# Low parts of the feed-forward's middle activations on DVE instead of GpSimd, in a two-layer decoder step

## What is computed

```python
def _swiglu(x, w_i, w_o):
    h = jnp.einsum('btd,df->btf', x, w_i)
    gate, up = h[..., :D_FF], h[..., D_FF:]
    return jnp.einsum('btf,fd->btd', jax.nn.silu(gate) * up, w_o)
...
yp = _layernorm(ALPHA * yp + 0.5 * _swiglu(yp, ffn1_wi[l], ffn1_wo[l]), ln_g[l, 0], ln_b[l, 0])
```

## Time and profile before

| | us |
|---|---|
| median of 3 runs | 1996.91 (1996.44 to 1997.46) |
| the profiled execution | 1998.58 |
| its span in the trace | 1996.8 |

### The profile page before, as it was taken

The page is one execution under the profiler, slowest core; times in us unless marked ns, Lnnn a source line. Parts: engine busy times, 40 slices in busy tenths (PEclk is TensorE's granted clock), DMA queues, the critical chain, the costliest instruction groups (busy, mean ns, idle before and its releaser), DMA issues.

```text
span 1996.8 us, 36337 instructions
## 1 busy us (share of the span) xinstructions
PE 1866.5 (93%) x14532; PEld 1786.2 (89%) x14532; DVE 1257.3 (63%) x1871; ACT 880.1 (44%) x1377; POOL 455.4 (23%) x340
## 2 busy tenths in 40 slices
PE   7999989999989869899999999999999689999996
PEld 7999989996966549899999999999998589999995
DVE  5888852446957413888872368888324788887223
ACT  4455531343334422655562264555513375556223
POOL 3000072151321344300026230000721430002520
PEclk9999999999989979899999999999999789999998
DMA  5333363271100223233333223333233123333221
GB/s 164 85 105 105 105 242 101 70 180 43 45 2 1 54 74 107 60 89 105 105 101 101 88 72 87 103 105 105 96 101 94 28 64 99 101 101 111 84 75 43
DMA packets 260087, 179.80 MB, mean 90 GB/s; under 512 B 10847, under 2 KB 256999, under 8 KB 259462
## 3 DMA queue, kind: packets, MB, share of 16 engines
q1 hardware_dynamic: 249952, 154.90, 26.6%
q0 software_dynamic: 2288, 13.54, 1.9%
q10 hardware_dynamic: 7742, 9.88, 1.8%
HBM read 169.62 MB, written 8.08 MB: 89 GB/s over the span
## 4 chain that ended last, share of the span: by engine, by line
PE 78%; DVE 8%; issue 7%; ACT 4%; POOL 2%; DMA 1%; ACTq 0%; POOLq 0%; DVEq 0%
PE ps L1116 39%; PE ps L1023 28%; PE ps L1203 3%; PE ps L1044 1%; DVE w_lo L1619 1%; PE ps L1208 1%; ACT w_hi L604 1%; PE ps L1093 1%; ACT xf L633 1%; ACT xh L631 1%; PE ps L1187 1%; POOL k_sel L2319 1%; PE ps L1282 1%; DVE xf L1651 1%; POOL diag L2331 1%
## 5 line engine op out<-in xcount | busy, mean ns | idle before, releaser
L1619 DVE TENSOR_TENSOR w_lo<-w_raw,w_hi 128x2048 fp32r<-128x2048 f32 (+1 forms) x70 | 183.8, 2628 | 286.7 <-ACT w_hi L604 286.7
L2267 POOL TENSOR_TENSOR hl<-hid_all,hh 128x520 fp32r<-128x520 f32 x88 | 134.3, 1562 | 850.2 <-ACT hh L889 850.2
L1023 PE MATMUL ps<-hh,w_hi 128*128 128x260 f32 x1408 | 295.2, 285 | 5.3 <-DVE w_lo L1619 5.3
L1023 PE MATMUL ps<-hh,w_lo 128*128 128x260 f32 x1408 | 293.8, 284 | 0.0
L604 ACT CAST w_hi<-w_raw 128x2048 fp32r<-128x2048 f32 (+1 forms) x70 | 126.2, 1804 | 247.5 <-PE ps L1023 229.9
L1023 PEld LDWEIGHTS ps<-hh,w_hi 128*128 128x128 f32 x1408 | 226.0, 190 | 5.7 <-DVE w_lo L1619 5.5
L1023 PEld LDWEIGHTS ps<-hh,w_lo 128*128 128x128 f32 x1408 | 226.0, 190 | 0.1
L2111 DVE TENSOR_TENSOR w_lo<-w_sum,w_hi 128x1024 fp32r<-128x1024 f32 x160 | 195.0, 1219 | 1.2 <-ACT w_hi L849 1.2
L849 ACT CAST w_hi<-w_sum 128x1024 fp32r<-128x1024 f32 x160 | 167.6, 1047 | 55.3 <-DVE w_sum L2094 55.1
L1116 PE MATMUL ps<-xh,w_hi 128*128 128x260 f32 x640 | 162.5, 286 | 18.9 <-ACT hid_all L863 16.1
L1023 PE MATMUL ps<-hl,w_hi 128*128 128x260 f32 x1408 | 178.0, 283 | 0.0
(11 more groups left out here) (327 smaller groups left out, 4457.3 us busy)
## 6 DMA issues: line engine op xcount, KB each, us to landing
w_raw<-in_ffn_wi_dram SPq DMA_DIRECT2D x176, 512.0 KB
w_raw<-in_ffn_wo_dram SPq DMA_DIRECT2D x32, 1024.0 KB
w_raw<-in_ffn_wo_dram SPq DMA_DIRECT2D x16, 768.0 KB
w_raw<-in_attn_w_in_dram SPq DMA_DIRECT2D x8, 1024.0 KB
keys_scratch<-key_half POOLq DMA_DIRECT2D x2, 2048.0 KB, 10.5
w_raw<-in_attn_w_o_dram SPq DMA_DIRECT2D x4, 1024.0 KB
x_in<-in_x_prompt_dram ACTq DMA_DIRECT2D x4, 512.0 KB, 9.8
out_dram<-y_out ACTq DMA_DIRECT2D x4, 512.0 KB
```

What stands on the lines that cost most here:

```text
L1023: mm = nc.tensor.matmul(ps[0:mc, bank + 2 * m + h, 0:HT], w[:, k, m, 0:mc], x(k)[:, h * HT:(h + 1) * HT], start=first and k == 0 and w is ...
L1619: nc.vector.tensor_tensor(w_lo[:, c % 2, 0:n], w_raw[:, c % 2, 0:n], w_hi[:, c % 2, 0:n].bitcast(F32), ALU.subtract).then_inc(s_lo, 1)
L2267: nc.gpsimd.tensor_tensor(hl[:, k, :], hid_all[:, k, :], hh[:, k, :].bitcast(F32), ALU.subtract).then_inc(s_hl, 1)
```

## The change

The subtraction `hl = hid_all - hh` moves from POOL to DVE, for all 22 tiles of each of the four feed-forwards, 88 instructions in all. On DVE tiles 0 to 4 stand between `hidden(KF - 2)` and the last gate addition; tiles 5 to 21 stand behind the split of chunk D1, which was already the next in DVE's order, and ahead of the split of D2. Line numbers below L2118 stay; behind it they move by 6, behind L2202 by 9, and on POOL those behind `hidden_lo` by 3.

```diff
@@ dve
+            def hidden_lo(st, begin, end):
+                for k in range(begin, end):
+                    dve.wait_ge(s_hh, st.hid + k + 1)
+                    nc.vector.tensor_tensor(hl[:, k, :], hid_all[:, k, :], hh[:, k, :].bitcast(F32), ALU.subtract).then_inc(s_hl, 1)
...
                 hidden(st, f, KF - 2)
+                hidden_lo(st, 0, EARLY)
                 gate(st, f, KF - 1, 1)
                 up(st, f, KF - 1)
                 hidden(st, f, KF - 1)
+                split_lo(st.chunk + KF + 1)
+                hidden_lo(st, EARLY, KF)
                 for g in range(4):
                     for n in range(3):
-                        if g < 3 or n < 2:
+                        if (g < 3 or n < 2) and (g, n) != (0, 0):
                             split_lo(st.chunk + KF + 3 * g + n + 1, 0, 1536 if n == 1 else CHUNK)
@@ pool
-                hidden_lo(st, 0, EARLY)
                 if name == "f0":
                     pool.wait_ge(s_used, 2 + st.chunk + KF)
                     for h in range(2):
                         fetch_half(h)
-                hidden_lo(st, EARLY, KF)
-                if name == "f0":
                     for h in range(2):
                         keep_half(h)
                     pool.wait_ge(s_kept, 32)
```

More of the change, by code:

```diff
@@ L2261, in sums @@
                     nc.gpsimd.tensor_tensor(sum_sq[:], sum_sq[:], sq[:, d % 2, :], ALU.add).then_inc(s_sum, 1)
[L2263 to L2267, removed]
             def fetch_half(h):
```

## The result

| | us |
|---|---|
| changed kernel, median of 5 runs | 2009.7 (2005.66 to 2011.54) |
| kernel before, median of 5 runs beside them | 1996.91 (1996.14 to 1997.46) |
| ratio | 1.0056, 95% interval 1.0045 to 1.0068 |
| profiled execution of the changed kernel, and its span | 2005.66, span 2003.9 |

The change makes the kernel slower, by 12.8 us on these medians. Three later measurements of the same two kernels gave 9.6 us (ratio 1.0051, 1.0034 to 1.0068), 12.7 us (1.0060, 1.0048 to 1.0072) and 11.1 us (1.0051, 1.0035 to 1.0068). I predicted slower, but by 4.5 us, and a range up to 2005.5 us, which the median is outside of.

A forecast was written before the change was run, and what follows sets the result against it. The prediction took PE, busy for 93% of the span, as the bound. Hold-up removed -8.1, gate delay +7.8 and slow clock +4.8 sum to +4.5 us on 1996.9, so 2001.4 us, range 1997.0 to 2005.5.

The forecast's parts named there:

- Part 1: Seventeen late subtractions off POOL end DVE's hold-up before D2 in f0: 8.1 us gained, if nothing else is late next.
- rival A: In f0 DVE's seventeen subtractions delay POOL's second key fetch, so PE waits before D4: 2009.5 us, chance 0.07.
- Part 2: Five early subtractions delay the last gate addition by 1.94 us in each of four feed-forwards: 7.8 us lost.
- Part 3: PE's clock falls behind the longer gate waits, likeliest at three of four places, 1.6 us each: 4.8 us lost.
- The rule against the row: Port-lock rule allows D2's split some 1.3 us of delay; the profile row shows 13.4 us, which the forecast followed.
- rival E: Something other than POOL's train holds DVE's D2 split, so f0's hold-up stays: 2009.5 us, chance 0.03.
- Rival B: None to two clock falls behind the gate waits, so no change: near 1998.5 us, chance 0.22.
- Rival C: The clock falls behind all four gate waits: +6.1 us, 2003.0 us, chance 0.25.
- Rival D: The five early subtractions cost the gate nothing, leaving only the f0 gain: 1988.8 us, chance 0.05.

The follow-up runs named there:

- late_keep: Kernel before with the seventeen late subtractions on DVE, five early ones left on POOL, f0's key stores held until D3's weights landed: 1994.08 us, ratio 0.9973.
- both: Changed kernel with the early five behind the last gate addition and f0's key stores held until D3's weights landed: 1989.37 us, on repeat 1988.63 us.
- three_ahead: Changed kernel with f0's key stores behind D3's weights, three early subtractions ahead of the last gate addition and two behind it: 1994.97 us, ratio 0.9978.
- early_only: Kernel before with only the five early subtractions moved to DVE, ahead of the gate; the seventeen late ones stay on POOL: 2015.57 us, ratio 1.0078.
- gate_first: Changed kernel with the five early subtractions on DVE behind the last gate addition: 1992.80 us, ratio 0.9969 to the kernel before.
- keep_late: Changed kernel with POOL's f0 key stores held until D3's weights landed: 2009.14 us, on repeat 2010.21 us.
- late_only: Kernel before with only the seventeen late subtractions moved to DVE; the five early ones stay on POOL: 1997.98 us, ratio 0.9992.
- fetch_behind: Kernel before with POOL's two f0 key fetches moved behind its seventeen late subtractions: 2017.64 us, one run.
- again_2: Changed kernel, unaltered, measured again: 2012.60 us, ratio 1.0060 to the kernel before.

## Why the prediction was wrong in size and right in sign

**Part 1, right in its size, wrong in "if nothing else is late next".** The hold-up of DVE went away, and with nothing else late f0's down part is 8.1 us shorter (late_keep, both, three_ahead), to the tenth what the comparison of f0 with f1 had given. But the changed kernel got 3.6 us of it. The step that failed is the condition I put on it without asking which transfer is late next. I had both numbers in hand: by rival A's own sum the stores would start by 274, some 8 us sooner (the first started at 269.01, 12.8 us sooner), and D3's load would be issued 1.94 us later into the same DMA engines (it was 3.6 us, 263.22 against 259.62, with the slow clock in it). I worked out the stores' path to D4 (rival A) but not what they do to another load beside them. Its price is 4.5 us in the traces, and it is the largest part of the miss of 8.3 us (2009.7 against 2001.4). The clock term adds 0.8 us; the other 3.0 us are on the first medians alone (none to 3.0 over the four measurements), and no run shows where they go.

**Part 2, right in the wait.** 1.94 us later and a wait of 2.63 us, four times, to 0.01 us. The step of 0.61 us per subtraction held (3.05 us for five). early_only and gate_first agree. That no later slack takes it back holds from f1's gate to f2's (372.09 us in the changed kernel, 368.75 before: 3.34 us more, 1.94 + 1.4). From f2's to f3's it is 429.81 against 427.17, 2.64 us more, so 0.7 us came back somewhere in the stretch with the pooling mixer; where isn't shown.

**Part 3, right in kind, a little small.** I took three falls of 1.6 us, 4.8 us; it was four of 1.4 us, 5.6 us. Over seven traces of three kernels (the changed one four times, keep_late twice, early_only) the clock fell behind 27 of 28 gate waits of 2.63 us, never behind the four of 1.41 us, nor behind the 0.69 us ones of late_only, late_keep, fetch_behind and the kernel before. My chance of two in three to three in four at each place was too low: it came from three waits of other stages, behind other work. A cost of 1.4 us is nearly the shorter bound that I had taken (1.55 us); twice it was 2.8 us.

**The rule against the row.** The Trainium skill, "SBUF — State Buffer", section "SBUF: two separate sides", gives the shared port pair to the instruction that started first, for the whole of that instruction. Where the fetches stand behind the train, and in f1 to f3, the trace agrees with the strict reading: the split's delay is 1.1 us, about one POOL instruction of 1.3 us. Where they stand ahead of it, the delay was 13.4 us, and the rule doesn't tell it. The prediction went by the row, which was right for this kernel.

**Rival A, wrong in its mechanism, near in its place.** The fetches took 1.61 and 2.27 us to issue, as before (1.67 and 2.26 us), and PE didn't wait before D4. The store at 269.01, in the midst of DVE's seventeen, was issued in 0.61 us. So no starvation of POOL's DMAs is seen. Its time, 2009.5 us, is that of the result by accident. So is rival E's.

**Rival B** fell with the four slow stretches. **Rival C**, all four fall, is what happened at the gates; with 4 x 1.4 its time would be 2002.2 us, and with the 4.5 us at D3 2006.7 us. **Rival D** fell: the gate was delayed. **Rival E** fell: the D2 split took 1.75 us.

**The range.** It took in the clock and the step of the subtractions, each at its worst, but no transfer: with D3's 4.5 us added, its upper sum of 2005.2 would have come to 2009.7.

**A better version.** The whole change is a gain if the five early subtractions stand behind the last gate addition and the stores wait for D3's load: both, 1989.37 us (ratio 0.9959) and 1988.63 us (0.9946, 0.9933 to 0.9959), 9 to 11 us under the kernel before. Of that, 8.1 us come from f0 and 4 x 0.69 = 2.8 us from the gate wait, which disappears too, because `hidden` no longer runs beside a POOL subtraction (it takes 0.69 us in f0, where it took 1.80).

## What to carry to other kernels

Where an edit makes an engine free earlier, list what it issues next and every transfer that will then be in flight with it; an engine's train may have been what kept a store out of the way of a load that matters. Put new work on a shared engine behind the instruction for which PE waits, not ahead of it: here five subtractions of 0.61 us, for which nobody waited yet, cost 15 to 22 us on the medians ahead of the gate, and behind it PE had no gate wait at all. And price a wait of PE by what follows it: from 1.41 to 2.63 us the price of one gate wait went from 1.4 to 4.0 us in the traces. A single trace of such a kernel can be some microseconds off at places that the edit doesn't touch, so compare the same stretch in two traces of one kernel before giving such a difference a cause.

## What the runs showed of the hardware

- DVE's two-input subtraction was shut out by a train of POOL subtractions for 13.4 us when two indirect DMAs had been issued by POOL just ahead of the train, and for 0.9 to 1.1 us when they had not (fetch_behind, and f1 to f3 of every trace with the train). It stayed shut out until the train's end, 10 us past the second fetch's landing (258.07 + 13.7 = 271.8). Why the fetches matter is open; I tried no other DMA ahead of the train.
- A load of 1 MB took some 26 us from its issue (about 263) to its landing (288.9), while 8 MB of keys passed too, 345 to 406 GB/s in all. In the first 14.7 us the weights' queue moved 283 packets and 0.29 MB, that of the keys 355 packets and 5.29 MB: near the same number of packets, but a packet of keys is some 15 times as large. Held behind it, the same stores let the load land 11 us sooner.
- Behind the same program place and the same wait of 2.63 us the granted clock fell to 0.50 in 27 of 28 cases. Other places (806 to 811 us, and the waits of 2.47 and 2.46 us before D3, after which it fell in again_2 and not in late_only) go either way.
